# Expert rows dealt over sixteen partition groups, and three weight matrices fetched partly in pieces of eight partitions

## The reference

```python
lg = hf @ wg + bg;  grp = argmax(lg)                  # one of 4 groups per token
le = (hf @ we + be) of that group                     # 8 experts in it
top_v, top_i = lax.top_k(le, 2)                       # two experts per token
wts = softmax(top_v) * softmax(lg)[grp]
for e in 32 experts, on the tokens that chose e:      # 1024 x 512, 1024 x 512, 512 x 1024
    y = (silu(x @ w1[e]) * (x @ w3[e])) @ w2[e]
out[token] += wts * y
```

## Time and profile before

| | |
|---|---|
| median of three runs | 1746.08 us |
| profiled execution | 1748.94 us, of it span 1747.1 us |
| TensorE busy | 1615.1 us (92%) |
| VectorE, ScalarE, GpSimd busy | 672.4, 403.9, 176.4 us |
| DMA moved | 362.38 MB, mean 207 GB/s |
| expert stage | from about 1156 us to the end |

### The profile page before, as it was taken

The page is one execution under the profiler, slowest core; times in us unless marked ns, Lnnn a source line. Parts: engine busy times, 40 slices in busy tenths (PEclk is TensorE's granted clock), DMA queues, the critical chain, the costliest instruction groups (busy, mean ns, idle before and its releaser), DMA issues. The chain is left out here.

```text
span 1747.1 us, 37145 instructions
## 1 busy us (share of the span) xinstructions
PE 1615.1 (92%) x15961; PEld 1046.2 (60%) x15961; DVE 672.4 (38%) x1654; ACT 403.9 (23%) x897; POOL 176.4 (10%) x220
## 2 busy tenths in 40 slices
PE   6999999998999999999999999999999999997772
PEld 3444445886777776644444445567786776765661
DVE  3523324213667667766555365561000000000003
ACT  4100000002666666510100003121211121121112
POOL 1205000000111010000000000011111111111110
PEclk9999999998999999999999999999999999999996
DMA  9874233145101108424533172179999999999995
GB/s 341 250 224 109 80 96 122 50 142 151 52 3 44 32 2 250 137 86 127 152 105 88 31 289 85 60 292 395 381 378 393 388 380 392 390 397 401 402 377 222
DMA packets 163793, 362.38 MB, mean 207 GB/s; under 512 B 28847, under 2 KB 111399, under 8 KB 139019
## 3 DMA queue, kind: packets, MB, share of 16 engines
q1 hardware_dynamic: 141456, 316.12, 49.2%
q0 software_dynamic: 12656, 28.01, 6.1%
q10 hardware_dynamic: 9516, 15.85, 2.6%
HBM read 323.67 MB, written 48.50 MB: 213 GB/s over the span
## 5 line engine op out<-in xcount | busy, mean ns | idle before, releaser
L2781 PE MATMUL psum<-sb_m_xT,sb_m_ring 128*64 128x64 f32 (+2 forms) x4096 | 150.8, 234 | 24.2 <-issue 18.3
L2781 PEld LDWEIGHTS psum<-sb_m_xT,sb_m_ring 128*64 128x64 f32 x4096 | 147.2, 140 | 37.4 <-issue 36.2
L2665 DVE TENSOR_TENSOR sb_m_hT<-psum,sb_m_sg 128x256 f32<-128x256 f32 (+2 forms) x32 | 15.3, 477 | 311.5 <-PE psum L2781 311.5
L2530 ACT ACTIVATE sb_m_xT<-psum,sb_rowmod 128x64 f32<-128x64 f32 (+2 forms) x256 | 81.7, 424 | 213.5 <-PE psum L2769 213.5
L849 PE MATMUL psum<-sb_vD,sb_room 128*128 128x512 f32 x240 | 104.7, 592 | 0.2 <-DVE sb_vD L730 0.2
L2781 PE MATMUL psum<-sb_m_xT,sb_front 128*64 128x64 f32 (+2 forms) x2560 | 92.3, 232 | 12.1 <-issue 8.4
L2781 PEld LDWEIGHTS psum<-sb_m_xT,sb_front 128*64 128x64 f32 x2560 | 89.7, 138 | 20.0 <-issue 19.7
L1147 ACT ACTIVATE sb_d_probs<-sb_d_probs,sb_d_nmax 128x640 f32<-128x640 f32 (+7 forms) x128 | 92.9, 735 | 13.4 <-DVE sb_d_nmax L1188 12.8
L1714 PE MATMUL psum<-sb_w_o_sb,sb_room 128*128 128x512 f32 x192 | 87.3, 613 | 0.0
L2788 PE MATMUL psum<-sb_m_ring,sb_m_hT 128*64 128x512 f32 (+2 forms) x256 | 84.1, 611 | 3.2 <-DMA sb_m_ring<-in_exp_w_dram 1.6
L1120 PE MATMUL psum<-sb_vS,sb_room 128*64 128x65 f32 x2112 | 80.0, 226 | 0.3 <-ACT sb_room L1134 0.3
(11 more groups left out here) (413 smaller groups left out, 2509.2 us busy)
## 6 DMA issues: line engine op xcount, KB each, us to landing
sb_m_ring<-in_exp_w_dram SPq DMA_DIRECT2D x48, 2048.0 KB, 36.6
sb_front<-in_exp_w_dram SPq DMA_DIRECT2D x30, 2048.0 KB, 35.5
sb_rows<-in_exp_w_dram SPq DMA_DIRECT2D x18, 2048.0 KB, 36.4
sb_g_ada<-in_ada_w_dram SPq DMA_DIRECT2D x16, 1024.0 KB, 5.2
d_qk<-sb_n_b_sel ACTq DMA_DIRECT2D x20, 512.0 KB, 3.3
sb_front<-in_w_in_dram SPq DMA_DIRECT2D x16, 512.0 KB, 5.4
sb_front<-d_qk SPq DMA_DIRECT2D x15, 512.0 KB, 7.0
sb_n_b_sel<-in_w_in_dram SPq DMA_DIRECT2D x10, 512.0 KB, 8.5
```

Of the source, the lines that this page charges most:

```text
L2530: last = act.activation(dst[:, kk, 0:w], src, ACT.Identity, scale=k.rowmod[:, 0, kk:kk + 1], bias=k.rowmod[:, 1, kk:kk + 1])
L2781: mm = pe.matmul(k.psum[part, which, c * w:(c + 1) * w], view[:, kk, first:first + 2 * CAPS - 1:2], x[:, kk, 0:w], start=(kk == 0), stop=( ...
```

## The change

1. **Places within a block.** After `dest` is known, 27 VectorE instructions move each row: place p of a block becomes (p mod 16) x (capacity / 16) + p div 16, the capacity being 64, 80 or 112. So sixteen consecutive rows go to sixteen groups of 4, 5 or 7 partitions. In every second block (of 128 places) the groups are dealt from the last to the first.
2. **The first block.** Its own table does the same by a changed comparison row, `first_order` (one more VectorE instruction), and is 80 places wide instead of 128; so are its index and its gather.
3. **Weights in pieces.** Matrices 6, 7 and 9 (gate and up of block 2, gate of block 3) come as one transfer of partitions 0 to 63 and eight transfers of eight partitions each. `loads` counts 9 x 16 for them.

```diff
+CELL = 16
+EIGHT = 8
+UNEVEN = (6, 7, 9)
@@ stage_out, VectorE
+            per = CAPM // CELL
+            v.inc(stt(first_order[:, :].rearrange("p (e q) -> p e q", e=CELL),
+                      const(K_M128, per).unsqueeze(1).to_broadcast([P, CELL, per]), CELL / P,
+                      const(K_I128, CELL).unsqueeze(2).to_broadcast([P, CELL, per]), ALU.mult, ALU.add))
...
-            v.inc(tt(chosen.rowhot0, chosen.row0.unsqueeze(2).to_broadcast([P, NT, P]),
-                     const(K_I128, P).unsqueeze(1).to_broadcast([P, NT, P]), ALU.is_equal))
+            v.inc(tt(chosen.rowhot0, chosen.row0.unsqueeze(2).to_broadcast([P, NT, CAPM]),
+                     first_order[:, :].unsqueeze(1).to_broadcast([P, NT, CAPM]), ALU.is_equal))
@@ stage_moe, SyncE
-        loads = lambda b, i: 16 * ((3 * b + i) // RING + (0 if (3 * b + i) % RING < AHEAD else 1))
+        parts_of = lambda n: 1 + P // 2 // EIGHT if n in UNEVEN else 1
+        loads = lambda b, i: 16 * sum(parts_of(n) for n in range((3 * b + i) % RING, 3 * b + i + 1, RING) if n >= AHEAD)
+        uneven = [(0, P // 2)] + [(p, p + EIGHT) for p in range(P // 2, P, EIGHT)]
...
-                    sp.dma_start(*expert_matrix(w, bass.ds(e, 1), ring[slot_of(b, i)], i == 2)).then_inc(s_w[slot_of(b, i)], 16)
+                    dst, src = expert_matrix(w, bass.ds(e, 1), ring[slot_of(b, i)], i == 2)
+                    for lo, hi in uneven if n in UNEVEN else ((0, P),):
+                        sp.dma_start(dst[lo:hi], src[lo:hi]).then_inc(s_w[slot_of(b, i)], 16)
@@ stage_moe, GpSimd
-            pool.indirect_dma_start(xg[0][:, :], None, k.d_xn, bass.IndirectOffsetOnAxis(ap=idx_first[:, 0:1], axis=0),
+            own = slice(0, CAPM)
+            pool.indirect_dma_start(xg[0][own, :], None, k.d_xn, bass.IndirectOffsetOnAxis(ap=idx_first[own, 0:1], axis=0),
@@ stage_moe, VectorE, after dest
+            v.inc(ts(cell, dest, 1.0 / CELL, 0.5 / CELL - 0.5, ALU.mult, ALU.add))
+            v.inc(ts(pair_of, dest, 1.0 / P, 0.5 / P - 0.5, ALU.mult, ALU.add))
...
+            v.inc(stt(step, wider, float((CAPW - CAPM) // CELL), narrow, ALU.mult, ALU.subtract)); v.wait(dve)
...
+            v.inc(stt(dest, turn_no, 1.0 - CELL, dest, ALU.mult, ALU.add)); v.wait(dve)
+            v.inc(tt(lane, lane, back, ALU.add)); v.wait(dve)
+            v.inc(stt(lane, step, float(CAPM // CELL), lane, ALU.add, ALU.mult)); v.wait(dve)
+            v.inc(tt(dest, dest, lane, ALU.add)); v.wait(dve)
```

More of the change, by code:

```diff
@@ L1817, in stage_out @@
         m1, u5 = sb("m1", [P, BANK])[:, :], sb("u5", [P, BANK])[:, :]
+        first_order = sb("first_order", [P, CAPM])
         s1, s2 = sb("s1", [P, HK, P])[:, :, :], sb("s2", [P, HK, P])[:, :, :]
@@ L2289, in __init__ @@
         self.rank, self.keyc, self.row0 = part(1), part(1), part(NT)
-        self.rowhot0 = rows[:, 1, :].rearrange("p (t r) -> p t r", t=NT)
+        self.rowhot0 = rows[:, 1, 0:NT * CAPM].rearrange("p (t r) -> p t r", t=NT)
         self.be_i = k.sbuf(ctx, "be_i", [1, NE], I32)
@@ L2345, in stage_moe @@
         dest, quot, unit, row = (scratch(2, NT) for _ in range(4))
+        cell, pair_of, narrow, past, wider, lane, turn_no, upper, step, odd, back = (scratch(2, NT) for _ in range(11))
         rowhot = ys[0][:, :].rearrange("p (j r) -> p j r", j=2 * NT)
@@ L2598, in _ @@
             dve.wait_ge(s_table0, 1)
-            v.inc(ts(pad0, k.psum[:, 3, 0:1], 0.0, const(K_PAD, 1), ALU.is_equal, ALU.mult)); v.wait(dve)
-            v.inc(stt(real0, k.psum[:, 3, 0:1], -1.0, pad0, ALU.add, ALU.add)); v.wait(dve)
-            dve.tensor_copy(idx_first[:, :], real0).then_inc(s_idx0, 1)
+            own = slice(0, CAPM)
+            v.inc(ts(pad0[own], k.psum[own, 3, 0:1], 0.0, k.const[own, K_PAD:K_PAD + 1], ALU.is_equal, ALU.mult)); v.wait(dve)
+            v.inc(stt(real0[own], k.psum[own, 3, 0:1], -1.0, pad0[own], ALU.add, ALU.add)); v.wait(dve)
+            dve.tensor_copy(idx_first[own, :], real0[own]).then_inc(s_idx0, 1)
             dve.wait_ge(s_start, 1)
@@ L2745, in _ @@
             for t in range(NT):
-                mm = pe.matmul(k.psum[:, 3, 0:1], chosen.rowhot0[:, t, :], k.const[:, K_TOK1 + t:K_TOK1 + t + 1],
+                mm = pe.matmul(k.psum[0:CAPM, 3, 0:1], chosen.rowhot0[:, t, :], k.const[:, K_TOK1 + t:K_TOK1 + t + 1],
                                start=(t == 0), stop=(t == NT - 1))
```

20 lines of the change are left out of this document (added).

## The result

The changed kernel takes 1780.37 us in the median of four runs (1772.93 to 1785.37). The kernel before took 1747.07 us beside it. The ratio is 1.0192, 95% interval 1.0171 to 1.0212: slower by about 33 us. The forecast was 1738.0, so the direction was wrong.

What follows compares the result with a forecast made beforehand. The weight stream was taken as the bound, ending late on unequally loaded engines. Stream -12 + 3.9 = -8.1 us, SyncE, VectorE and start 0, gave 1738.0 us from the median 1746.08; range 1731 to 1747.

Steps and rivals of the forecast that it cites:

- The bound: Expert stage: the weight stream sets the program's end until 1690 us, with 23.6 us of TensorE work and a tail behind.
- Rows: Row transfers load engines unequally; the latest is 12 us late against an even load, and spreading rows wins that.
- Three matrices in pieces: Matrices 6, 7, 9: pieces shift 15.8 us between engine halves, leaving the latest 3.9 us behind the mean; later landings cost 0.
- a weight wait before 1300 us: Sign of a wrong forecast: TensorE waiting for weights this early would mean the pieces came too late.
- The other one: Sign of a wrong forecast: end-of-stream share still falling over 20 us, from engines' own pace or pieces on the wrong half.
- the late group: At the stream's end, roughly five engines finishing near 1710 us, 8 us after the bulk; taken to lie in the relieved half.
- the late group lies in the half that the pieces load: Rival on the stream's end: -12 + 11.9, so 1746.0 us, no change; chance 0.12, of which 0.01 slower.
- VectorE: 27 added instructions before the table take 3.9 us; 1.9 hidden, 2.0 delay TensorE, absorbed by weight waits: 0 at the end.
- SyncE: Issue of 16 more pieces takes 9.9 us, 3.2 us of cover remain; matrix 10 issued 1.4 us late; cost 0.
- Deal the pieces over all engines: Rival on the pieces: no load shift, 4 us left over instead of 3.9, the same 1738 us; no chance of its own.
- pile on one: Rival on the pieces: all on one engine, 126 us on it, costing over 100 us; within the 0.08 for slower by own pace.
- The chance of slower at 0.09: Whole kernel: 0.08 for engines' own pace (1754 us) with the pile of pieces, 0.01 from the loaded late group.

Runs made afterwards that it cites:

- e1: The changed kernel with rows spread, but matrices 6, 7 and 9 each whole in one transfer: 1737.6 us, ratio 0.9946 to the kernel before.
- e5: The changed kernel with matrices 6, 7 and 9 each in two transfers of 64 neighbouring partitions, nothing in eights: 1757.6 us, ratio 1.0055 to the kernel before.
- e3: The changed kernel, but each piece of the upper half takes eight partitions 4 apart instead of eight neighbours: 1765.1 us, ratio 1.0105 to the kernel before.
- e15: The changed kernel with the upper half of matrices 6, 7 and 9 in four transfers of 16 partitions 4 apart: 1752.6 us, ratio 1.0051.
- e12: The changed kernel with only matrix 6 cut: twelve pieces of 8 partitions 12 apart, one of the last 32: 1749.7 us, ratio 1.0017.
- e13: The changed kernel with matrices 6, 7 and 9 each in four transfers of 32 partitions 4 apart over the whole height: 1737.1 us, ratio 0.9939.
- e9: The changed kernel with matrices 6, 7 and 9 each in four transfers of 32 neighbouring partitions: 1753.2 us, ratio 1.0032 to the kernel before.

## Why the prediction was wrong

**The bound: right.** The stream sets the end in both kernels.

**Rows: right in size, in part by luck.** The forecast was -12 us with 4 left over, so -8; e1 measured -8.8. The lateness of the last part was 11.7 us before, as forecast, but 7.9 are left over with even rows, not 4: the step that the forecast had read from the share remains, as two groups of eight parts, 8.3 us apart at their edges and 12.4 by their means. By the windows the tail's loss fell from 10.4 to 5.9 us, 4.5 of it. The rest came from a term that the forecast did not have: the rate from 1260 to 1560 rose from 387 to 391 GB/s, 300 x 4 / 391 = 3.1 us more. TensorE's weight waits from 1560 to 1692 fell only from 15.2 to 9.2 us where about 5 were forecast, and the median landing from 36.6 to 34.4 us:

```profile
sb_m_ring<-in_exp_w_dram SPq DMA_DIRECT2D x48, 2048.0 KB, 34.4
```

**Three matrices in pieces: this step failed.** It said that the eight engines with the pieces "do 12 rows' work instead of 8 and the others 4, plus and minus 2.6 us a matrix", and that later landings of matrices 6, 7 and 9 cost 0. It priced a row at the time that a row of a whole matrix takes, wherever it is written. The sum had 3.9 us left over for the pieces and the rows together, where 4 stood for the rows alone, so nothing for the pieces; measured they cost 42.8 us (1780.4 - 1737.6). In the profiled executions the last landing is 37.4 us later (586.4 against 549.0): 31.4 on all engines, the time of the bytes missing in the slow stretch, and 6.0 in a later last part. In place of the failed step the runs showed three things.
- The lower half, a transfer that looks harmless, already runs at half rate, as the upper half would: e5 costs 20.0 us with no pieces at all, 16.1 by its last landing. By rates, three matrices at 213 instead of 391 GB/s are 6.29 MB x (1 / 213 - 1 / 391) = 13.4 us.
- Eight neighbouring partitions reach two groups of sixteen: 8 KB took 1.10 us of an engine instead of 0.34. Against pieces 4 apart this is 15.3 us (1780.4 - 1765.1).
- Eights cost more than their place explains (e3 against e15, e12), about half of it in the uneven end.

The landings were late by 12.9, 25.5 and 37.9 us instead of up to 7.9, and TensorE still had no weight wait for them: it started on matrix 6 at 1222.2, on 7 near 1226.9 and on 9 at 1243.0, after each had landed, and its first weight wait came at 1318. So that part of the step held, and the sign "a weight wait before 1300 us" did not come. The other one did: the share falls over 24 us. The stream ended later although nobody waited: bytes not moved while it is the bound are not made up. "Landing later costs 0 where nobody waits" holds for a transfer that is delayed behind others, not for one that takes the engines' time from all that follow.

**The uneven load can be seen, and it worked against the kernel.** The forecast took the late group to lie in the relieved half and left the latest part 3.9 us behind the mean. It lies 13.9 us behind: two parts come alone and last. So the rival "the late group lies in the half that the pieces load" was true for two of eight parts, if the reading above holds.

**VectorE: right. SyncE: right only for matrices 6 and 7.** 2.4 us stood for 2.0. 3.0 us of cover were left for 3.2, by luck in its parts: an issue took 0.75 us instead of 0.62, and the table came 18.9 us behind the first issue instead of 16.3. Matrix 10 was issued 15.2 us later than forecast, since the issues of matrix 9 took up to 6.2 us each. No loss from that is seen at a share of 1.02.

**The rivals.** None named the partitions written to. "Deal the pieces over all engines" and "pile on one" asked which engine reads its work, not where it writes. The Trainium skill's rule for whole, large transfers (DMA: Bandwidth & Descriptors, rules for kernel authors) stood against the pieces with an estimate of 48 us for them, +40 in the sum, and I set it aside because issues do not wait for landings. The size came close to the 42.8 us, by luck. The fixed cost for each transfer that the estimate was made of (fitted there on transfers of the software queue) does not show: e13 has twelve transfers of 512 KB for three matrices and loses nothing against the rows alone. The map on the Trainium skill's page SBUF — State Buffer, not weighed in the prediction, gives the lower half half the rate at once; e5 and e9 agree (204 to 215 GB/s in the windows shown, against 391). The chance of slower at 0.09 was far too low for a part whose rate no row of the trace before showed.

## What to carry to other kernels

Before a transfer is cut by partitions, count how many of the sixteen groups (four neighbouring partitions, the same again 32 on) each part reaches. Cut it by steps over the height, such as even and odd or every fourth: these lost nothing here. Parts of eight partitions cost more than their place and unbalance the engines. Read GB/s beside the DMA share: a share of 1.0 says that engines are occupied, not that they move bytes at their rate. Where a change has two parts, the good one should be timed alone: here it was worth 0.5% and was buried by the other.

## What the runs showed of the hardware

- 64 neighbouring partitions: 209 to 211 GB/s; 32 neighbouring: 204 to 215; 64 every second or 32 every fourth: 387 to 390 over 72 us, gathers included, as whole matrices (389).
- The loss is on the side of SBUF: 4 apart in SBUF gains 15.1 us over 4 apart in DRAM (1766.9 against 1782.0).
- Not expected: eight partitions 12 apart, eight groups for eight engines, still ran at 230 to 253 GB/s with the rest of the traffic; sixteen 4 apart on the eight groups of the upper half cost no more than halves. About half of what eights cost beyond that is the uneven end (two parts last, alone by 6 to 12 us); the rest is not explained.
- With rows and transfers even, the last matrix still lands in two groups of eight parts, 8 to 10 us apart, in all seven such runs.
- While the pieces were in flight, an issue on SyncE took up to 6.2 us, against 0.37 to 0.38 with whole matrices.
